# Order of the first loads in a hybrid attention layer: one weight block in two transfers, token rows ahead of the last two blocks, and two small moves in the step schedule

## The chip, the cores and the metric

The kernel runs on one core of a Trainium2 chip. The metric is the device time of one launch in microseconds (us). One execution was also recorded by the hardware profiler; all rows of a trace in this text come from that execution.

The engines are named as in the profile: PE is TensorE (PEld its weight loads, PEq its sequencer), DVE is VectorE, ACT is ScalarE, POOL is GpSimd, SP is SyncE. SP computes nothing here: it only issues transfers, in program order. A transfer that SP issues travels in queue q1; an indirect gather that POOL issues travels in queue q0. Both queues use the same 16 DMA engines.

## What is computed

One inference step of one decoder layer for 512 prompt tokens and 8 decode rows (each with a past of 4096 tokens in paged caches), all in float32:

```python
xn = _rmsnorm(x, norm_pre)
(qa, kvc, kvs, kvw, gn, ga, qd, kvd, krp, gb, ma, mb) = jnp.split(xn @ w_in, IN_OFFSETS, axis=-1)
...
o_a   = gg[..., 0:1] * o_c + gg[..., 1:2] * o_s + gg[..., 2:3] * o_w   # compressed, selected, sliding
o_lat = _mla_attend(q_lat, q_pe, t, c, kr, pos_k)                      # multi-head latent attention
...
pa = (o_a * jax.nn.silu(ga)) @ w_proj_a
pb = (o_b * jax.nn.silu(gb)) @ w_proj_b
h = jax.nn.sigmoid(ma) * pa + jax.nn.sigmoid(mb) * pb
return x + _rmsnorm(h @ w_out, norm_post)
```

For the decode rows the compressed branch averages blocks of 32 cached tokens. The whole compressed cache of those rows, 32 MB, is read for that.

## The kernel before, in words

Every engine has one program written out by hand, and semaphores order the engines. Three stretches matter here.

**Projection, about 0 to 134 us.** The 520 token rows stand transposed in `XG`, as 8 blocks of 128 channels (`k` = 0 to 7). The attention columns of `w_in` are 1976 wide and lie in `W` in two halves of 988; each half has 8 blocks `k` of 128 x 988 words (494 KB), and each block two pieces `n` of 494 columns. A tile is 128 tokens. `project_first` (L957) works on tiles 0 and 1 with the first half: for each `k` it waits for `xg` (`XG` block scaled by DVE in `scale_x`) and for `w_in{k}`, then makes four products of 494 columns. Then `project(u)` (L970) for `u` = 2 to 7 takes one tile and one half each, `u` = 4 to 7 being the second half. A bank is free for the next tile once ACT (`evict`) and DVE (DVE's own `project`, for the first two tiles) have copied it out (`tiles_evicted`). The copy multiplies by 1/rms of the token, which comes from the token rows as such: SP loads them into `xtok` (2 MB) and `xdec`, ACT squares them, and a short chain of DVE and ACT gives `inv_root`. PE starts with two products on zeros (L1060).

SP issues, in this order: `XG` block 0, `W` block 0, `XG` 1 and 2, `W` 1, `W` 2, `XG` 3 and 4, `W` 3, `W` 4, `XG` 5 to 7, `W` 5, `W` 6, `W` 7, then the token rows (L645, L646). After that it waits for `summed` 1, and issues the second half of the weights (L650).

**The gathers, inside the projection.** POOL waits for `w_in7`, and then issues 32 indirect gathers of 1 MB of the compressed cache (L821). There are six slots; gather g+6 waits until DVE has made the first sum of gather g (`summed`, L2065). DVE reduces each gather in three additions (L2065, L2067, L2071; the last raises `sum1`). DVE's order is: eviction of tile 0, gathers 0 and 1, eviction of tile 1, gathers 2 to 7, and so on. PE takes them up in `average(b)` (L1004), which waits for `sum1` of 4(b+1) and stands at fixed places in PE's program: `average(0)` is in tile `u` = 2, `average(1)` in `u` = 3, `average(2)` in `u` = 4. PE works in order, so that a wait in `average` holds all products behind it.

**After the gathers.** POOL gathers rotary keys, SP writes them out again turned (`rope_out`, L662), and only then SP issues `w_qup` and `w_k` (L667, L668), for which ACT waits at L1788 before it copies the columns `ROPE_W` and evicts the transposed queries that PE needs at L1110.

**Attention steps, about 184 to 450 us.** 48 steps `d`, each with two attention units of the prompt. The latent attention of the decode rows is spread over them by hand: `latent_pair(p2, d, d2)` puts the scores of 8 pages at step `d` and of 8 more at `d2`; softmax is at `d2`, the outputs at `d2` + 1. The rotary keys of a pair are loaded to one place (`KRR`) by an ACT transfer, which waits until the pair before has used it (`load_rope`, L1818). `G_at` lists the steps at which PE computes one of 16 gate halves (L1398), eight products of 260 columns.

Of the kernel before, what the change touches and what calls it, by code (L numbers as in the profile page):

```python
# [16 lines left out]
P = 128  # L17
D_MODEL = 1024
SEQ = 512
DEC = 8  # L20
# [13 lines left out]
TILES = SEQ // P  # L34
KM = D_MODEL // P
TOK = SEQ + DEC
# [6 lines left out]
GW = W_ATTN // NG  # L43
# [120 lines left out]
def build(nc, t):  # L164

    ctx = ExitStack()
    with ctx:
# [14 lines left out]
        S = Sems()  # L182
# [10 lines left out]
        W = sb("W", NG * 8 * GW)  # L193
        XG = sb("XG", KM * TOK + 24)
        OA = sb("OA", 5 * 512)
        OB = sb("OB", 5 * 512)
        VV = sb("VV", TILES * 256)
# [6 lines left out]
        rope_rows = nc.dram_tensor("rope_rows", (16 * P, 4 * P), F32, kind="Internal").ap()  # L204
        bank = [ctx.enter_context(nc.psum_tensor(f"bank{i}", [P, 512], F32)) for i in range(8)]
# [35 lines left out]
        xtok, xdec, sqs = c_(4096), c_(1024), c_(1024)  # L241
# [95 lines left out]
        ROPE_APART = (13, 15)  # L337

        def rope_home(p2):
            return PTd[:, :] if p2 in ROPE_APART else KRR[:, 0:512]  # L340

        def rope_landed(eng, p2):
            if p2 in ROPE_APART:
                eng.wait_ge(S["rope_apart"], 16 * (ROPE_APART.index(p2) + 1))
            else:
                eng.wait_ge(S["kr_landed"], 16 * sum(1 for x in range(p2 + 1) if x not in ROPE_APART))

# [67 lines left out]
                C_at[d + 1] = add(d + 1, "slc", r, 0, 512, 4, 64, n, r, False, J_SLC + r)  # L415
                C_at[d + 2] = add(d + 2, "slc", r, 1, 512, 4, 64, n + 1, n, True, J_SLC + r)

        for p2, (d, d2) in enumerate(((0, 1), (3, 4), (6, 7), (9, 10), (12, 13))):
            latent_pair(p2, d, d2)
        for g in range(6):  # L420
            latent_pair(5 + g, 15 + 4 * g, 16 + 4 * g)
            cached(g, 21 if g == 1 else 16 + 4 * g)
        for p2, d in ((11, 39), (12, 41), (13, 43), (14, 45), (15, 47)):
            latent_pair(p2, d, d + 1)
        G_at = {d: i for i, d in enumerate((23, 25, 26, 27, 29, 30, 33, 34, 35, 37, 38, 41, 43, 45, 48, 49))}
        APPLY_at = {d: (i,) for d, i in G_at.items() if i < 14}
        APPLY_at[PAIRS + 1] = (14, 15)
        TURN_IN_7 = {d for d in SOFT_at if d >= 16}
# [148 lines left out]
        def w_part(half, k, n):  # L577
            at = ((half * KM + k) * 2 + n) * GW
            return W[:, at:at + GW]
# [58 lines left out]
        def _(sp):  # L638
            for k in range(KM):
                if k in X_RUNS:  # L640
                    r = X_RUNS.index(k)
                    k2 = (*X_RUNS, KM)[r + 1]
                    sp.dma_start(XG[:, k * TOK:k2 * TOK], t["xT"][:, k * TOK:k2 * TOK]).then_inc(S[f"xT_in{r}"], 16)
                sp.dma_start(W[:, k * 2 * GW:(k + 1) * 2 * GW], t["w_attn"][:, k, 0:2 * GW]).then_inc(S[f"w_in{k}"], 16)
            sp.dma_start(xtok.rearrange("p (t c) -> p t c", t=TILES), t["x"][0:SEQ].rearrange("(t p) c -> p t c", p=P)).then_inc(S["xtok_in"], 16)  # L645
            sp.dma_start(xdec[0:DEC], t["x"][SEQ:TOK]).then_inc(S["xtok_in"], 16)  # L646

            sp.wait_ge(S["summed"], 1)
            for k in range(KM):
# [153 lines left out]
            for i, tl in enumerate(ROWS_DONE):  # L803
                for hf in range(2):
                    sp.wait_ge(S["y"], 2 * i + hf + 1)
                    c = slice(hf * 512, (hf + 1) * 512)
# [130 lines left out]
        def _(pe):  # L937
# [19 lines left out]
            def project_first():  # L957
                for k in range(KM):
                    pe.wait_ge(S["xg"], k + 1)
                    pe.wait_ge(S[f"w_in{k}"], 16)  # L960
                    for tl in range(2):
                        for n in range(2):
                            mm = pe.matmul(bank[2 * tl + n][:, 0:GW], XG[:, k * TOK + tl * P:k * TOK + (tl + 1) * P],
                                           w_part(0, k, n), start=(k == 0), stop=(k == KM - 1))
                        if k == KM - 1:
                            mm.then_inc(S["p1"], 1)
                    if k == 2:
                        pages()
# [87 lines left out]
                mm.then_inc(S["group_dec"], 1)  # L1056

            pe.wait_ge(S["pe_zero"], 1)
            for _ in range(2):
                pe.matmul(bank[7][:, :], VV[:, 0:P], VV[:, 0:512], start=True, stop=True)  # L1060
            project_first()
            for u in range(2, 8):
                project(u)
# [25 lines left out]
            for b in range(4):  # L1089
                for e in range(2):  # L1090
                    n = 4 * e + b
                    mm = pe.matmul(bank[5][32 * e:32 * e + 32, 0:P], QZraw[:, n * 64 + 32 * e:n * 64 + 32 * e + 32], KcT[:, n * P:(n + 1) * P],
                                   start=(b == 0), stop=(b == 3))
# [15 lines left out]
            for k in range(4):  # L1109
                mm = pe.matmul(bank[2][32 * k:32 * k + 32, :], kcBD[:, (k // 2) * 32:(k // 2 + 1) * 32], qTraw[:, k * 512:(k + 1) * 512],  # L1110
                               start=True, stop=True)
# [5 lines left out]
            for n in range(10, 16):  # L1117
                c, w = GROUPS[n]
                mm = pe.transpose(bank[7][0:w, P + 8 * n:P + 8 * n + 8], projD[0:DEC, c:c + w], ident8)
# [63 lines left out]
            for b in range(4):  # L1183
                for e in range(2):
                    n = 4 * e + b
# [463 lines left out]
        def _(act):  # L1649
# [159 lines left out]
            def load_rope(p2):  # L1809
                if p2 == ROPE_APART[0]:  # L1810
                    act.wait_ge(S["do_ps"], sum(1 for c in chunks if c["kind"] != "mla"))
                elif p2:
                    act.wait_ge(S["ds"], mla[p2 - 2 if p2 > ROPE_APART[0] else p2 - 1]["q"] + 1)
                else:
                    act.wait_ge(S["pooled"], 8)
                    act.wait_ge(S["rope_out0"], 128)
                    act.wait_ge(S["rope_out1"], 128)
                act.dma_start(rope_home(p2), rope_rows[p2 * P:(p2 + 1) * P]).then_inc(S["rope_apart" if p2 in ROPE_APART else "kr_landed"], 16)  # L1818

            group_copied(act, 15)  # L1820
            for i in range(4):
# [1141 lines left out]
```

## Time and profile before

| | |
|---|---|
| median of 3 runs | 666.37 us (666.15 to 666.65) |
| profiled execution, device time | 666.29 us |
| its span in the trace | 664.5 us |
| PE busy | 650.8 us, 98% of the span |
| DVE busy | 446.0 us, 67% |
| ACT busy | 214.4 us, 32% |
| DMA, mean | 270 GB/s over the span; 396 GB/s in the first 60 us |

The span starts at the first recorded instruction; the device time has 1.8 us around it. A row of the timeline reads: start, duration, engine, line, operation, tensors, count, and in brackets how long the engine was idle before and what ended it.

### The profile page before, as it was taken

Reading aid. Unit: us, or ns where it says so; the run is one execution under the profiler, and the core shown is the slowest. Engines: PE = TensorE matmul, PEld = TensorE weight load, DVE = VectorE, ACT = ScalarE, POOL = GpSimd, SP = SyncE. Lnnn points to the kernel's source line nnn. Section 1 sums busy time; section 2 is a strip of 40 time slices with the busy share of each in tenths; the row PEclk is TensorE's granted clock in tenths of the full one; section 3 lists DMA queues with packets and bytes.
Section 4 is the critical chain, followed back from the end, with each engine's and each line's share of the span. In section 5 each row is a group of like instructions: output and inputs, shape, how many; then the busy total and the mean of one; then the engine's idle time right before and its main releaser. Section 6 shows DMA issues by size and latency. Waiting matters only on the chain.

```text
span 664.5 us, 15351 instructions
## 1 busy us (share of the span) xinstructions
PE 650.8 (98%) x5771; PEld 433.3 (65%) x5771; DVE 446.0 (67%) x1234; ACT 214.4 (32%) x586; POOL 77.6 (12%) x89
## 2 busy tenths in 40 slices
PE   8999999999999998999999999999999999999996
PEld 3444444463466775778777676688788888886443
DVE  2198799676677778866575664637585757648866
ACT  0311321686445455544453542421011111010221
POOL 0344334126000000220201000000000000000010
PEclk9999999999999999999999999999999999999998
DMA  8999999999989999978759789975411112018011
GB/s 332 417 425 422 423 427 403 353 379 273 366 277 381 400 399 412 408 276 326 279 177 373 276 318 359 406 270 222 159 64 64 64 49 78 1 70 343 3 64 63
DMA packets 67587, 179.44 MB, mean 270 GB/s; under 512 B 7513, under 2 KB 16498, under 8 KB 60218
## 3 DMA queue, kind: packets, MB, share of 16 engines
q1 hardware_dynamic: 56088, 125.14, 51.2%
q0 software_dynamic: 8640, 48.90, 18.2%
q10 hardware_dynamic: 2786, 4.42, 1.8%
q8 instruction: 46, 0.75, 0.4%
q14 instruction: 27, 0.22, 0.1%
HBM read 169.38 MB, written 12.72 MB: 274 GB/s over the span
## 4 chain that ended last, share of the span: by engine, by line
PE 88%; DVE 5%; DMA 3%; ACT 2%; issue 1%; SPq 1%; DVEq 0%; ACTq 0%
PE bank L1561 20%; PE bank L978 12%; PE bank L1398 9%; PE bank L1612 7%; PE bank L1259 5%; PE bank L1382 4%; PE bank L1285 4%; PE bank L1269 4%; PE bank L1367 4%; DMA projP<-x 3%; PE bank L1590 2%; PE bank L1142 2%; PE bank L1332 2%; PE bank L1342 1%; PE bank L1220 1%
## 5 line engine op out<-in xcount | busy, mean ns | idle before, releaser
L978 PE MATMUL bank<-W,XG 128*128 128x494 f32 x192 | 83.6, 580 | 0.7 <-DVE projP L1998 0.7
L1871 ACT ACTIVATE projP<-bank,projP 128x128 f32<-128x128 f32 (+3 forms) x96 | 49.8, 525 | 38.5 <-DVE projP L2354 37.8
L2657 DVE TENSOR_TENSOR projP<-projP,bank 128x260 f32<-128x260 f32 x81 | 32.6, 422 | 42.4 <-PE bank L1561 41.6
L1398 PE MATMUL bank<-W 128*128 128x260 f32 x256 | 60.3, 389 | 0.0
L1661 ACT ACTIVATE projP<-bank 128x128 f32<-128x128 f32 (+5 forms) x87 | 33.4, 392 | 82.2 <-PE bank L1561 47.7
L978 PEld LDWEIGHTS bank<-W,XG 128*128 128x128 f32 x192 | 35.2, 192 | 36.5 <-issue 35.0
L1398 PEld LDWEIGHTS bank<-W 128*128 128x128 f32 x256 | 47.3, 190 | 10.6 <-issue 3.5
L1661 ACT ACTIVATE W<-bank 128x512 f32<-128x512 f32 (+2 forms) x69 | 40.2, 582 | 38.3 <-PE bank L1021 13.3
L2354 DVE CUSTOM_DVE_ANT_0 bank<-bank,maskb 128x128 f32<-128x128 f32 (+3 forms) x96 | 45.6, 509 | 8.0 <-PE bank L1259 7.1
L1259 PE MATMUL bank<-W 64*128 64x128 f32 (+7 forms) x192 | 46.0, 466 | 0.7 <-ACT projP L1871 0.7
L821 POOL DMA_INDIRECT ring<-cmp,idxi x32 | 38.6, 1208 | 67.8 <-DVE VV L2065 48.1
L2065 DVE TENSOR_TENSOR VV<-ring 128x1024 f32<-128x1024 f32 x32 | 39.1, 1222 | 7.6 <-DMA ring<-cmp,idxi 5.2
L881 POOL TENSOR_TENSOR ring<-XG,OB 128x512 f32<-128x512 f32 x3 | 3.8, 1270 | 300.7 <-DVE XG L2755 300.7
L1561 PE MATMUL bank<-ring 128*128 128x260 f32 x168 | 38.2, 383 | 0.0
L1269 PE MATMUL bank<-cst,projP 128*128 128x128 f32 x240 | 36.7, 280 | 0.3
L1561 PEld LDWEIGHTS bank<-ring 128*128 128x128 f32 x168 | 31.8, 190 | 5.3 <-issue 0.4
L1561 PE MATMUL bank<-W 128*128 128x260 f32 x144 | 34.6, 383 | 0.0
L1952 ACT ACTIVATE projP<-projP 128x260 f32<-128x260 f32 x28 | 11.3, 420 | 71.0 <-DVE projP L2657 70.9
L1269 PEld LDWEIGHTS bank<-cst,projP 128*128 128x128 f32 x240 | 26.7, 140 | 9.7 <-issue 5.0
L1999 DVE TENSOR_SCALAR projP<-projP,sm 128x128 f32<-128x128 f32 (+3 forms) x64 | 28.6, 447 | 2.3
L1561 PEld LDWEIGHTS bank<-W 128*128 128x128 f32 x144 | 27.2, 190 | 4.1
L1612 PE MATMUL bank<-ring,W 128*128 128x512 f32 x64 | 28.3, 592 | 0.0
(479 smaller groups left out, 1163.6 us busy)
## 6 DMA issues: line engine op xcount, KB each, us to landing
ring<-latent SPq DMA_DIRECT2D x168, 256.0 KB, 4.9
XG<-latent SPq DMA_DIRECT2D x56, 256.0 KB, 4.4
W<-w_gate SPq DMA_DIRECT2D x12, 1024.0 KB, 5.8
W<-w_attn SPq DMA_DIRECT2D x16, 494.0 KB, 12.2
W<-latent SPq DMA_DIRECT2D x20, 256.0 KB, 5.3
rope_rows<-ring SPq DMA_DIRECT2D x16, 256.0 KB, 4.4
ring<-win SPq DMA_DIRECT2D x8, 512.0 KB, 7.7
ring<-w_out SPq DMA_DIRECT2D x2, 2048.0 KB, 11.8
```

The source lines that it names most:

```text
L821: pool.indirect_dma_start(out=dst, out_offset=None, in_=src, in_offset=bass.IndirectOffsetOnAxis(ap=rows, axis=0)).then_inc(sem, 16)
L978: mm = pe.matmul(bank[2 * (u % 2) + n][:, 0:GW], XG[:, k * TOK + tl * P:k * TOK + (tl + 1) * P], w_part(half, k, n), start=(k == 0), stop= ...
L1259: pe.matmul(bank[x % 2][:, 0:width], q, kk, start=True, stop=True).then_inc(S["s"], 1)
L1269: mm = pe.transpose(pt_bank(u)[:, kb * P:(kb + 1) * P], Pb[u % 4][:, kb * P:(kb + 1) * P], ident)
L1398: mm = pe.matmul(bank[6][:, 0:HALF], gate_w[g % 2][:, at:at + P], X2[:, k * TOK + hf * HALF:k * TOK + (hf + 1) * HALF], start=(k == 0), st ...
L1561: mm = pe.matmul(pair_bank(v, name)[:, 0:HALF], stationary(a, kk), moving(b, kk), start=(kk == 0), stop=(kk == inner - 1))
L1612: mm = pe.matmul(bk[:, lo:hi], lhs, rhs, start=(kk == 0), stop=(kk == 3))
L1661: return act.activation(dst, src, ACT.Copy, scale=scale)
L1871: act.activation(Pb[u % 4][:, 0:w], bank[u % 2][:, 0:w], ACT.Exp, bias=NMp[:, u:u + 1], scale=-1.0, accum_out=RSp[:, u:u + 1]).then_inc(S[ ...
L2065: dve.tensor_tensor(sum4, x[:, 0:1024], x[:, 1024:2048], ALU.add).then_inc(S["summed"], 1)
L2354: dve.tensor_tensor_reduce(bank[u % 2][:, 0:w], bank[u % 2][:, 0:w], maskb[:, 512 - w:512], -1.0, 1e38, ALU.add, ALU.min, NMp[:, u:u + 1]) ...
L2657: dve.tensor_tensor(out, a, pair_bank(v, product)[:, 0:HALF], ALU.add).then_inc(S["z_by_dve"], 1)
```

## The change

Four edits. (1) `W` block 0 is loaded as two transfers of 247 KB, the second with a semaphore of its own (`apart_in`, which also takes over the counts of `rope_apart`); `project_first` makes the two products with the first piece, waits, and makes the two with the second. (2) The token rows are issued between `W` 5 and `W` 6 instead of after `W` 7. (3) The second product on zeros has 256 columns instead of 512. (4) The second half of latent pair 2 moves from step 7 to step 8 (its softmax to step 8 and its outputs to step 9), and gate half 13 from step 45 to 46.

```diff
-                eng.wait_ge(S["rope_apart"], 16 * (ROPE_APART.index(p2) + 1))
+                eng.wait_ge(S["apart_in"], 16 * (ROPE_APART.index(p2) + 2))
...
-        for p2, (d, d2) in enumerate(((0, 1), (3, 4), (6, 7), (9, 10), (12, 13))):
+        for p2, (d, d2) in enumerate(((0, 1), (3, 4), (6, 8), (9, 10), (12, 13))):
...
-        G_at = {d: i for i, d in enumerate((23, 25, 26, 27, 29, 30, 33, 34, 35, 37, 38, 41, 43, 45, 48, 49))}
+        G_at = {d: i for i, d in enumerate((23, 25, 26, 27, 29, 30, 33, 34, 35, 37, 38, 41, 43, 46, 48, 49))}
...
-                sp.dma_start(W[:, k * 2 * GW:(k + 1) * 2 * GW], t["w_attn"][:, k, 0:2 * GW]).then_inc(S[f"w_in{k}"], 16)
-            sp.dma_start(xtok.rearrange("p (t c) -> p t c", t=TILES), t["x"][0:SEQ].rearrange("(t p) c -> p t c", p=P)).then_inc(S["xtok_in"], 16)
-            sp.dma_start(xdec[0:DEC], t["x"][SEQ:TOK]).then_inc(S["xtok_in"], 16)
+                if k == 6:
+                    sp.dma_start(xtok.rearrange("p (t c) -> p t c", t=TILES), t["x"][0:SEQ].rearrange("(t p) c -> p t c", p=P)).then_inc(S["xtok_in"], 16)
+                    sp.dma_start(xdec[0:DEC], t["x"][SEQ:TOK]).then_inc(S["xtok_in"], 16)
+                if k == 0:
+                    sp.dma_start(W[:, 0:GW], t["w_attn"][:, 0, 0:GW]).then_inc(S["w_in0"], 16)
+                    sp.dma_start(W[:, GW:2 * GW], t["w_attn"][:, 0, GW:2 * GW]).then_inc(S["apart_in"], 16)
+                else:
+                    sp.dma_start(W[:, k * 2 * GW:(k + 1) * 2 * GW], t["w_attn"][:, k, 0:2 * GW]).then_inc(S[f"w_in{k}"], 16)
...
-                    for tl in range(2):
-                        for n in range(2):
-                            mm = pe.matmul(bank[2 * tl + n][:, 0:GW], XG[:, k * TOK + tl * P:k * TOK + (tl + 1) * P],
-                                           w_part(0, k, n), start=(k == 0), stop=(k == KM - 1))
-                        if k == KM - 1:
+                    for tl, n in ((0, 0), (1, 0), (0, 1), (1, 1)) if k == 0 else ((0, 0), (0, 1), (1, 0), (1, 1)):
+                        if (k, tl, n) == (0, 0, 1):
+                            pe.wait_ge(S["apart_in"], 16)
+                        mm = pe.matmul(bank[2 * tl + n][:, 0:GW], XG[:, k * TOK + tl * P:k * TOK + (tl + 1) * P],
+                                       w_part(0, k, n), start=(k == 0), stop=(k == KM - 1))
+                        if k == KM - 1 and n == 1:
                             mm.then_inc(S["p1"], 1)
...
-            for _ in range(2):
-                pe.matmul(bank[7][:, :], VV[:, 0:P], VV[:, 0:512], start=True, stop=True)
+            for width in (512, 256):
+                pe.matmul(bank[7][:, 0:width], VV[:, 0:P], VV[:, 0:width], start=True, stop=True)
```

## Rows read from the trace of the kernel before

**Rows 1.** The page: span, and busy time of each engine.
```profile
span 664.5 us, 15351 instructions
PE 650.8 (98%) x5771; PEld 433.3 (65%) x5771; DVE 446.0 (67%) x1234; ACT 214.4 (32%) x586; POOL 77.6 (12%) x89
```
**Rows 2.** Busy time by stretch (stretch, its length, then each engine), 60 to 130 us.
```profile
60.00:130.00 70.00, 70.00 (x351) 32.04 (x349) 59.30 (x98) 24.89 (x55) 23.57 (x20) 1.00 1.01 402
```
**Rows 3.** The chain of waits that ended last, first 60 us.
```profile
8.05 17.59 DMA projP<-x
```
**Rows 4.** PE's timeline after the first two tiles.
```profile
34.06 11.85 PE L978 MATMUL bank<-W,XG 128*128 128x494 f32 x28 [0.70 <-DVE projP L1998]
```
**Rows 5.** PE instructions of two lines, first 35 us: ns min/median/max, first and last start.
```profile
L1060 PE MATMUL bank<-VV x4: 1061/1061/1222, 1.5 to 4.2; 128*128 128x512 f32 x4
...
L963 PE MATMUL bank<-W,XG x64: 575/577/768, 5.5 to 32.8; 128*128 128x494 f32 x64
```
**Rows 6.** SP's transfers: `XG` block 0 to landing; `W` 0 to 7, issue and landing.
```profile
XG<-xT SPq DMA_DIRECT2D x1, 260.0 KB, 3.0
...
L644 SPq DMA_DIRECT2D W<-w_attn x8: 417/479/707, 1.2 to 6.9; - x8
...
DMA to landing us min/median/max: 4.2/9.7/13.1
```
**Rows 7.** DMA queues (packets, MB, share): 23.5 to 24, 24 to 38, 38 to 62 us.
```profile
q1 hardware_dynamic: 49, 0.16, 79.4%
q0 software_dynamic: 8, 0.07, 32.2%
...
q0 software_dynamic: 794, 5.85, 100.2%
...
q0 software_dynamic: 927, 6.72, 66.6%
```
**Rows 8.** Timeline: the first gather, SP's second half of the weights.
```profile
20.87 1.01 POOL L821 DMA_INDIRECT ring<-cmp,idxi  x1 [18.14 <-DMA W<-w_attn]
...
35.07 4.38 SPq L650 DMA_DIRECT2D W<-w_attn  x8
```
**Rows 9.** Issue to landing: gather 7 (issued at 37.83 us), gather 11 (at 48.32).
```profile
ring<-cmp,idxi POOLq DMA_INDIRECT x1, 10.4
...
ring<-cmp,idxi POOLq DMA_INDIRECT x1, 15.3
```
**Rows 10.** Timeline: last addition of gather 7, `average(1)`, gather 11, `average(2)`.
```profile
54.26 0.42 DVE L2071 TENSOR_TENSOR KRR<-VV 128x256 f32<-128x256 f32 x1
...
56.55 0.41 PE L1011 MATMUL bank<-OA,cst 128*32 128x256 f32 x2
...
63.68 1.23 DVE L2065 TENSOR_TENSOR VV<-ring 128x1024 f32<-128x1024 f32 x1 [1.26 <-DMA ring<-cmp,idxi]
...
71.42 0.40 PE L1011 MATMUL bank<-KRR,cst 128*32 128x256 f32 x1
```
**Rows 11.** Timeline: last addition of gather 19, `average(4)`.
```profile
92.19 0.42 DVE L2071 TENSOR_TENSOR KRR<-VV 128x256 f32<-128x256 f32 x1
...
94.84 0.41 PE L1011 MATMUL bank<-OA,cst 128*32 128x256 f32 x2
```
**Rows 12.** Timeline: `w_qup` issued, ACT's first copy of it, PE behind it.
```profile
126.66 0.66 SPq L667 DMA_DIRECT2D ring<-w_qup  x1
...
138.56 0.73 ACT L1661 ACTIVATE KRR<-ring 128x256 f32<-128x256 f32 x2
...
140.88 1.06 PE L1110 MATMUL bank<-W,XG 128*32 128x512 f32 x8 [0.16 <-ACT XG L1738]
```
**Rows 13.** The transfer issued right behind `w_k`, at 127.85 us: to landing.
```profile
ring<-const SPq DMA_DIRECT2D x1, 512.0 KB, 15.1
```
**Rows 14.** Timeline: outputs in step 8, the gate half of step 45.
```profile
213.94 0.86 PE L1285 MATMUL bank<-projP,W 128*32 128x128 f32 x24 [0.46 <-DVE projP L2362]
...
422.23 3.77 PE L1398 MATMUL bank<-W 128*128 128x260 f32 x16
```

More of the change, by code:

```diff
@@ L1817, in load_rope @@
                     act.wait_ge(S["rope_out1"], 128)
-                act.dma_start(rope_home(p2), rope_rows[p2 * P:(p2 + 1) * P]).then_inc(S["rope_apart" if p2 in ROPE_APART else "kr_landed"], 16)
+                act.dma_start(rope_home(p2), rope_rows[p2 * P:(p2 + 1) * P]).then_inc(S["apart_in" if p2 in ROPE_APART else "kr_landed"], 16)
             group_copied(act, 15)
```

## Prediction

> **What bounds the kernel now.** I read the page first: PE is busy for 98% of the span [rows 1], so a change gains only where PE waits or starts late, and costs wherever it makes PE wait. Busy time by stretch says the same of the part this change touches: from 60 to 130 us PE is busy for 70.00 of 70.00 us [rows 2]. Then the chain of waits for the first 60 us: its longest piece is the transfer of the token rows, issued at 8.05 and awaited for 17.59 us, to 25.6 [rows 3]. Behind it come five squares, the root, and the first evictions, and PE's timeline shows the price: 0.70 us idle before tile 2, released by DVE's eviction [rows 4]. With the start of the first real product at 5.51 [rows 5] these are the two places where PE is late. Last I read the DMA queues and the gathers, since the token rows are put ahead of something that others wait for.
>
> **Edits 1 and 3, the start.** `XG` block 0 landed at 0.76 + 3.0 = 3.8, `W` block 0 at 1.2 + 4.2 = 5.4 [rows 6]. Half of the block should land half of that interval earlier, at about 4.6. The shorter second product on zeros leaves PE free in time: each of the 4 instructions has 1061 ns [rows 5], half the columns save some 0.43 us in each of two, so they end at 4.4 rather than 5.25. PE starts up to 0.86 us earlier. But the products of 512 zeros at 1061 ns and the later ones of 494 columns at 577 ns [rows 5] stand for the two levels of the clock, 1.2 and 2.4 GHz, although the record of the granted clock shows full speed throughout; the first real product, 768 ns, still has the change in it. So the level rose just after 5.5, and what is done before that goes at half speed: the gain is 0.43 (bounds 0 and 0.86).
>
> **Edit 2, what it gains.** The token rows are no longer behind `W` 6 and 7, 1.0 MB, 2.4 us at the 0.418 MB/us of a full queue (5.85 MB in 14 us, [rows 7]). `inv_root` comes before tile 0 is done, and the 0.70 us go [rows 4]. Blocks 6 and 7 land 5.1 us later, at 23.9 and 25.1, and PE wants them at about 26 and 29: covered. Without anything else the change would gain 0.43 + 0.70 = 1.1 us.
>
> **Edit 2, what it costs.** POOL starts its gathers only when `W` 7 has landed: it landed at 6.9 + 13.1 = 20.0 [rows 6], and the first gather was issued at 20.87, released by it after 18.14 us [rows 8]. The token rows are 2.13 MB, 2.13 / 0.418 = 5.1 us of the queue. `W` 7 then lands at 25.1 and the first gather is issued at 26.0. Its first bytes were seen 2.8 us after the issue (8 packets of q0 between 23.5 and 24, [rows 7]), so they come at about 28.8. Before, the token rows filled q1 during just this latency. Now nothing is behind `W` 7: SP waits for `summed` 1, which waits for the first gather. The DMA engines stand idle from about 24.2 to 28.9, 4.7 us, in a stretch where they were full.
>
> The Trainium skill (DMA: Bandwidth & Descriptors, Queues, rings and completion order) says that each DMA engine consumes a ring's descriptors in ring order, and that completion need not be in order. By the landings, 4.2 to 13.1 us after issue in the order of issue, the trace agrees with the first part; if the engines overtook one another, `W` 7 would land earlier than I say. The same page (Specifications) gives about 1 us to the first byte on the POOL path. This trace has 2.8 us, and the measurement decides; by 1 us, as an estimate from that page, the hole would be 2.9 instead of 4.7 us, and the time 668.9.
>
> **Who is short of data.** Gather g is in when q0 has moved (g + 1) x 1.05 MB. Before, q0 moved 0.07 + 5.85 = 5.92 MB by 38 us, alone, and from then 6.72 / 24 = 0.280 MB/us beside the second half of the weights [rows 7]. Test on gather 7: 8.39 MB at 38 + 2.47 / 0.280 = 46.8; it landed at 37.83 + 10.4 = 48.2 [rows 9], 1.4 later. Gather 11: 61.8, landed at 63.6 [rows 9], 1.8 later. Now after the change. q0 starts at 28.9. Gather 0 lands at 28.9 + 2.5 + 1.4 = 32.8, DVE's first addition ends at 34.0, and SP issues the second half of the weights then instead of at 35.07 [rows 8]. Their bytes began 2.9 us after that issue, so the sharing begins at 36.9 with 3.34 MB moved.
> - Gather 7: 36.9 + 5.05 / 0.280 + 1.4 = 56.3. DVE's three additions take 2.4 us (1.23 the first, 0.42 the last, [rows 10]), so `sum1` 8 is there at 58.7. `average(1)` ran at 56.55, with 1.9 us to spare since 54.68 [rows 10]. PE reaches it at 55.4 and waits 3.3 us: 2.1 us later than before.
> - Gather 11: 36.9 + 9.24 / 0.280 + 1.8 + 2.4 = 74.1, against `average(2)` at 71.42 [rows 10]. PE comes at 73.6 and waits again: **2.7 us later** than before. Both gains of PE at the start are inside this wait and count nothing.
> - From there the gathers are late by the whole hole, 4.7 us, and PE by 2.7. `average(4)` had 94.84 - 92.61 = 2.2 us to spare [rows 11]; 4.7 - 2.7 = 2.0 fits in it just. The cost of a miss is what is missing, 0 to 0.5 us; I take 0.
>
> **The next in line.** SP issues `w_qup` and `w_k` after the rotary rows, which come after the gathers, at 126.66 [rows 12]; now 4.7 later. ACT copied from it at 138.56 with no wait in the row, and PE waited 0.16 us at L1110 for the evictions that follow on ACT [rows 12], so there is no cover on that side. The transfer right behind `w_k` landed at 127.85 + 15.1 = 142.95 [rows 13], half a megabyte later, so `w_k` landed not long before 138.5. If just then, ACT waits 4.7 - 2.7 = 2.0 us; if 2 us earlier, nothing. Being nearer to the first, I take **1.5 us**. Queued behind ACT's wait are the evictions of the transposed queries, and PE waits for them. What follows is timed by PE again.
>
> **Edit 4.** Before, PE waits 0.46 us in step 8 for DVE [rows 14], while step 7 carries eight more pages. Moving them (1.3 us of PE) fills that hole and leaves step 7 with 1.3 us less cover for the softmax of its wide units. Outputs and the slot of those pages come a step later, and the next rotary load starts some 4 us later with one step less to land. Gain 0.5, loss 0.5: I take 0. Gate half 13 is 3.8 us of PE work in step 45 [rows 14]; the neighbours have it as cover or not, both steps being full of PE work. Its weights are long in, and SP's loads don't count it. 0, between -0.2 and 0.2.
>
> **Sum.** 2.7 + 1.5 = 4.2 us on the execution of 666.29 us, whose span is 664.5: 670.5. The median of the runs, 666.37, is 0.1 above that execution, so nothing is to be corrected.
>
> **The rivals.** (a) The hole costs at the two averages alone, since `w_k` was in early enough, or the second wait is smaller: 666.3 + 2.1 to 2.7 = 669.0. For it: no row shows when `w_k` landed. (b) The hole is short, since the gather's first bytes come sooner on an empty queue, as after the page's 1 us: +2.6, 668.9. Against it: 2.8 us in this trace. (c) On the other side: the gathers keep up. If POOL's gathers start so early, or DVE has so much in hand, that gather 7 is added by 55.4 and gather 11 by 70.3, PE keeps its 1.1 us: 665.2. It decides if the gathers come less than 0.7 us later than before at gather 7; for it speaks that all the bytes are the same and PE had 1.9 us to spare; against it, that DVE waited for gather 11 already, 1.26 us [rows 10]. (d) The waits just eat the gains: 666.3 +- 1.3, no change. (e) The clock: PE stands for 3.3 us before `average(1)`, more than anywhere in the record after the start. If the level falls to 1.2 GHz, each microsecond at it costs half of one. Only what exceeds the 0.5 us that PE comes early to `average(2)` counts, and it takes the place of the wait for `w_k`: up to 3 us more, 671 to 674. The Trainium skill (TensorE: Matmul & The Clock Gate, the HAM clock gate) says that the slow state is the default and activity lifts it; by that rule the fall is possible, and rows 5 agree for the start.
>
> **Chances.** Forecast 0.55 (its own range 669.3 to 672.0), (a) 0.15, (b) 0.05, (c) 0.12, (d) 0.06, (e) 0.07. The range leaves out (c), most of the low part of (d) and the far end of (e): 667.0 to 673.0. A measurement of this kernel can tell about 0.2%, 1.3 us, from no change: faster 0.12, same 0.07, slower 0.81.
>
> **What would show it.** In the trace after: no q0 or q1 bytes between 24.3 and 28.7; `W` 7 landing at about 25 and the first gather at 26; tile 2 following tile 1 on PE without the 0.70 us; PE idle 3 us before L1011 at 58.7 and again shortly at 74; ACT idle before its first copy from `w_qup`. If the first gather starts near 21, or DMA is full around 26, the prediction is wrong at its root. If PE doesn't wait at L1011, the model of the sharing is wrong; if L1110 is late by as much as `average(2)`, the 1.5 us are.

## The result, and the profile after

The changed kernel took 674.62 us, the median of 4 runs (673.43 to 676.06), beside 666.51 us for the kernel before (4 runs): a ratio of 1.0103, 95% interval 1.0066 to 1.014. The profiled execution took 673.43 us, with a span of 671.6 us: 7.1 us more than before, where I forecast 4.2. By the medians it is 8.1 us. The profiled execution is the shortest of the four; the other three have a lower granted clock (0.992 or 0.993 on the mean, beside 0.996) and no trace.

The page first: the span, and PE's share one point lower. PE is busy for 651.9 us rather than 650.8 [rows 1], so most of the 7.1 us is waiting and some is work at a lower speed.

```profile
span 671.6 us, 15352 instructions
...
PE 651.9 (97%) x5771; PEld 433.9 (65%) x5771; DVE 446.7 (67%) x1234; ACT 214.3 (32%) x586; POOL 77.7 (12%) x89
```

The summary of PE's waits (line waited for: us in total, times, longest) says where it stood. The first two lines are new.

```profile
PE bank L1017 <- DVE KRR L2077: 3.4, 1, 3.4
PE bank L1116 <- ACT XG L1744: 3.2, 1, 3.2
```

Lines behind the edits are numbered 5 or 6 higher than before. Busy time by stretch (the last three columns are granted clock, DMA share and GB/s) shows the cause of both:

```profile
20.00:24.00 4.00, 4.00 (x11) 1.89 (x10) 0.00 (x0) 0.64 (x1) 0.00 (x0) 1.00 1.03 374
24.00:28.00 4.00, 4.00 (x11) 1.83 (x10) 0.00 (x0) 3.91 (x8) 1.17 (x2) 1.00 0.13 53
28.00:32.00 4.00, 4.00 (x11) 1.77 (x10) 1.03 (x6) 1.41 (x4) 3.08 (x4) 1.00 0.92 305
32.00:36.00 4.00, 4.00 (x11) 1.90 (x10) 3.05 (x5) 1.34 (x2) 2.71 (x3) 1.00 0.96 360
60.00:130.00 70.00, 69.50 (x348) 31.95 (x341) 61.08 (x89) 24.28 (x55) 25.09 (x20) 1.00 1.00 410
```

The DMA engines ran dry between 24 and 28 us, as forecast, but they were also thin on both sides of it. The kernel before moved 415, 407, 428 and 430 GB/s in these four stretches; the difference is 2.35 MB, 5.6 us of a full queue, where I had counted 4.7. The timelines of POOL, SP, ACT and PE follow the delay down:

```profile
26.53 1.00 POOL L826 DMA_INDIRECT ring<-cmp,idxi  x1 [23.79 <-DMA W<-w_attn]
...
59.61 0.41 PE L1017 MATMUL bank<-OA,cst 128*32 128x256 f32 x2 [3.44 <-DVE KRR L2077]
...
75.05 0.40 PE L1017 MATMUL bank<-KRR,cst 128*32 128x256 f32 x1 [0.50 <-DVE OA L2077]
...
132.50 0.65 SPq L672 DMA_DIRECT2D ring<-w_qup  x1
...
145.24 0.72 ACT L1667 ACTIVATE KRR<-ring 128x256 f32<-128x256 f32 x2 [3.13 <-DMA ring<-w_k]
...
147.56 1.93 PE L1116 MATMUL bank<-W,XG 128*32 128x512 f32 x8 [3.22 <-ACT XG L1744]
```

Against [rows 8, 10, 12]: the first gather is 5.66 us later, `average(1)` 3.06, `average(2)` 3.63, the issue of `w_qup` 5.84, and L1116 6.68. The eight products at L1116 last 1.93 us instead of 1.06, and the granted clock says why. It is at 0.50, the 1.2 GHz level, once PE has stood idle for 3.2 us:

```profile
144.00:146.00 2.00, 0.35 (x4) 0.11 (x1) 1.97 (x9) 0.76 (x3) 0.40 (x1) 1.00 1.02 303
146.00:148.00 2.00, 0.44 (x4) 0.23 (x8) 0.76 (x2) 1.98 (x5) 2.00 (x4) 0.73 0.98 390
148.00:150.00 2.00, 2.00 (x11) 0.43 (x4) 0.00 (x0) 1.99 (x4) 0.15 (x1) 0.50 1.03 421
```

The transfers of 24 to 38 us in 40 slices of 0.35 us show the hole itself, with the first bytes again in the slice from 28.2:

```profile
GB/s 395 181 34 0 0 0 0 0 0 0 0 0 328 164 164 421 445 374 374 351 375 258 281 304 304 374 351 328 281 375 398 421 445 375 421 445 421 351 375 442
```

At the start the first product comes 1.20 us earlier than in [rows 5], and yet the gain is gone before the third block:

```profile
4.31 4.88 PE L969 MATMUL bank<-W,XG 128*128 128x494 f32 x8
9.42 6.87 PE L969 MATMUL bank<-W,XG 128*128 128x494 f32 x16 [0.23 <-DMA W<-w_attn]
...
17.09 16.75 PE L969 MATMUL bank<-W,XG 128*128 128x494 f32 x40
33.68 2.65 PE L984 MATMUL bank<-W,XG 128*128 128x494 f32 x6
```

The last 40 products of `project_first` began at 16.61 before and begin at 17.09 now. The 0.70 us of idle time before tile 2 [rows 4] are gone, so tile 2 is 0.38 us early in all.

The books of the profiled pair: +3.63 to `average(2)`, which stays to 133 us; +3.05 at the wait for `w_k` (L1116 is 6.68 late); +1.07 by the low clock behind it (the row at 170.12 was at 162.37, 7.75 in all); -0.6 later on. That is 7.1.

### The profile page after: what moved, and what is told of

Read it like the earlier page. It is cut to its first block, busy times and chain, and to the rows that moved or that the text cites. A ratio compares the mean times of both kernels' runs of the same rounds, so it can differ in the third digit from the quotient of the medians.

```text
span 671.6 us, 15352 instructions
## 1 busy us (share of the span) xinstructions
PE 651.9 (97%) x5771; PEld 433.9 (65%) x5771; DVE 446.7 (67%) x1234; ACT 214.3 (32%) x586; POOL 77.7 (12%) x89
## 4 chain that ended last, share of the span: by engine, by line
PE 73%; DMA 12%; DVE 9%; issue 2%; SPq 2%; ACT 1%; POOL 0%; DVEq 0%; POOLq 0%; ACTq 0%
PE bank L1567 20%; PE bank L1404 9%; PE bank L1618 7%; DMA ring<-cmp,idxi 7%; PE bank L1265 5%; PE bank L1388 4%; PE bank L1291 4%; PE bank L1275 4%; PE bank L1373 4%; DVE VV L2071 3%; DMA W<-w_attn 2%; PE bank L1596 2%; DMA ring<-w_k 2%; PE bank L1148 2%; PE bank L1348 2%
## 5 line engine op out<-in xcount | busy, mean ns | idle before, releaser
L984 PE MATMUL bank<-W,XG 128*128 128x494 f32 x192 | 83.5, 579 | 0.0
L969 PE MATMUL bank<-W,XG 128*128 128x494 f32 x64 | 28.5, 602 | 0.2 <-DMA W<-w_attn 0.2
```

The lines of the kernel that those rows point to most:

```text
L984: mm = pe.matmul(bank[2 * (u % 2) + n][:, 0:GW], XG[:, k * TOK + tl * P:k * TOK + (tl + 1) * P], w_part(half, k, n), start=(k == 0), stop= ...
```

## The experiments

Each kernel ran 6 to 13 times, beside the kernel before on the same chip. The medians of the kernel before were 665.67 us beside the first four rows of the table, 666.76 for the next four, 666.52 for the next four and 665.35 for the last four. The ratio is not the quotient of the two medians, and where they disagree the interval decides.

| kernel | median us | ratio | 95% interval |
|---|---|---|---|
| before, edit 2 alone | 671.64 | 1.0094 | 1.0056 to 1.0131 |
| after, edit 2 undone | 665.61 | 1.0005 | 0.9978 to 1.0032 |
| after, gathers from block 5 | 665.48 | 0.9995 | 0.9978 to 1.0012 |
| before, edit 4 alone | 666.18 | 0.9999 | 0.9978 to 1.0020 |
| before, gathers late | 671.40 | 1.0075 | 1.0049 to 1.0101 |
| before, edits 1 and 3 | 667.53 | 1.0008 | 0.9988 to 1.0029 |
| after, evictions first | 671.12 | 1.0069 | 1.0045 to 1.0093 |
| after, both waits filled | 673.48 | 1.0097 | 1.0077 to 1.0117 |
| after, again | 673.25 | 1.0088 | 1.0056 to 1.0119 |
| after, both waits filled, again | 672.91 | 1.0110 | 1.0046 to 1.0173 |
| after, one wait filled | 673.06 | 1.0088 | 1.0062 to 1.0114 |
| before, rows early, gathers from block 5, latent pair 2 moved | 666.02 | 0.9991 | 0.9962 to 1.0021 |
| the same, evictions first | 665.08 | 1.0001 | 0.9990 to 1.0011 |
| before, evictions first | 665.46 | 1.0004 | 0.9988 to 1.0019 |
| after, evictions first, again | 671.13 | 1.0088 | 1.0062 to 1.0115 |
| the same, first wait filled | 669.97 | 1.0070 | 1.0057 to 1.0083 |

**Which edit.** Edit 2 alone, put into the kernel before:

```
+                if k == 6:
+                    sp.dma_start(xtok..., t["x"][0:SEQ]...)
+                    sp.dma_start(xdec[0:DEC], t["x"][SEQ:TOK])
                 sp.dma_start(W[:, k * 2 * GW:...], t["w_attn"][:, k, 0:2 * GW])
-            sp.dma_start(xtok..., t["x"][0:SEQ]...)
-            sp.dma_start(xdec[0:DEC], t["x"][SEQ:TOK])
```

> The kernel before with edit 2 alone: token rows ahead of weight blocks 6 and 7, the first block in one transfer, both zero products of 512 columns, edit 4 left out. Theory (the hole in the DMA queues carries the loss, since the gathers wait for weight block 7): first gather issued near 26, average(1) near 59, average(2) near 75, the wait for w_k 3 us, and the time some 7.5 to 8 us above before, 674. Rival 1 (the split first block and its small packets delay the early blocks and so carry a part): 2 us or more less than that, 672 or below. Rival 2 (the loss comes from edit 4): within 1 us of before.

Taken out of the changed kernel, with all else left in:

> The changed kernel with edit 2 undone: the token rows are again issued behind weight block 7; the split first block, the short zero product and edit 4 stay. Theory (edit 2 carries the whole loss, edit 4 gives back the 0.6 us that the trace of after shows between 262 and 443 us, the start gives nothing): 665.8, that is 0.5 below before. Rival (the split first block costs, since block 1 landed 0.7 us later): 667 to 668. If it stays above 671, edit 2 isn't the cause.

Edit 4 alone, `(6, 7)` to `(6, 8)` and gate half `45` to `46`:

> The kernel before with edit 4 alone (second half of latent pair 2 from step 7 to step 8, gate half 13 from step 45 to step 46). Theory (the 0.6 us that after gives back between 262 and 443 us are PE's idle time before step 8's pages): 0.5 us below before, 665.9. Rival (they come from the shifted phase of the loads, not from edit 4): 0 within 0.2.

Edits 1 and 3 alone:

> The kernel before with edits 1 and 3 alone: first weight block in two transfers, second zero product of 256 columns. Theory (the level of the clock rises at the same time whatever is done before it, and block 1 lands 0.4 to 0.7 us later than PE wants it): the first real product starts near 4.3, the ninth at 9.4 to 9.6 rather than 9.02, tile 2 on PE is as late as before, and the time is within 0.4 us of before. My prediction's term: 0.43 us below before. Rival (small packets delay all of the start): 1 us or more above before.

Edit 2 alone costs 6.0 us by the medians; without it the changed kernel is at 665.61, level with before. I had expected 7.5 to 8 us from edit 2, and had given 672 or below as the sign that the split first block carries a part. 671.64 is below that line, but the other two runs speak against it: with the split block and edit 2 undone nothing is lost, and edits 1 and 3 alone measure +0.8 us within an interval that holds 0. A share of some tenths of a microsecond isn't excluded. My 0.43 us of gain isn't there. Edit 4 measures nothing: the 0.6 us of the profiled pair are below what the runs tell. The trace of edits 1 and 3 shows block 1 awaited, and its first product (the ninth of all) at 10.29, later than the 9.4 to 9.6 that I expected:

```profile
4.44 5.14 PE L968 MATMUL bank<-W,XG 128*128 128x494 f32 x8
10.29 6.87 PE L968 MATMUL bank<-W,XG 128*128 128x494 f32 x16 [0.71 <-DMA W<-w_attn]
...
17.96 16.75 PE L968 MATMUL bank<-W,XG 128*128 128x494 f32 x40
```

**Is it the hole?** The changed kernel, with one number changed: POOL's gathers wait for block 5, which is issued ahead of the token rows.

```
-            pool.wait_ge(S["w_in7"], 16)
+            pool.wait_ge(S["w_in5"], 16)
```

> The changed kernel, and POOL's first gather waits for weight block 5, which is issued ahead of the token rows, and no longer for block 7. All the data and the order on SP's queue stay. Theory (the loss is the hole): gathers are issued from about 16, no stretch without bytes, average(1) and average(2) run without a wait, w_k lands early enough, the time 665 to 666. Rival (token rows ahead of blocks 6 and 7 are dear by themselves, or sharing the engines with the gathers makes blocks 6 and 7 and the token rows late): PE waits at L969 or at the first eviction, and the time is 667 to 670.

And from the other side, the kernel before with its old order, and gathers that start late:

```
-            pool.wait_ge(S["w_in7"], 16)
+            pool.wait_ge(S["xtok_in"], 32)
```

> The kernel before, and POOL's first gather waits for the token rows in place of weight block 7. Order and sizes of all transfers stay; only the gathers start about 5.6 us later, when the queue has run dry. Theory (the lateness of the gathers is the whole cause, whatever order the token rows have): a stretch without bytes from about 25.5 to 28.5, PE waits 3 to 4 us at average(1), and the time is 5.5 to 8 us above before, like the kernel with edit 2 alone. Rival (the order of the token rows itself costs): less than 3 us above before.

The first takes the whole loss away (665.48 us), the second brings in 4.6 us of it with no transfer moved, below the 5.5 that I gave as the least. Its first gather went at 25.53, 1.0 us earlier than in the changed kernel; whether that is all of the difference isn't shown. From 24 to 32 us the two rows of the changed kernel above make 1.43 MB; with gathers from block 5 the queues stay full, and its first gather is out at 18.92 (not at 16, as expected: the row has it released by the last indices from DVE, not by the weights):

```profile
24.00:28.00 4.00, 4.00 (x11) 1.79 (x10) 0.00 (x0) 3.91 (x7) 1.83 (x2) 1.00 1.01 423
28.00:32.00 4.00, 4.00 (x11) 1.90 (x10) 1.02 (x6) 1.58 (x5) 0.00 (x0) 1.00 1.02 429
```

With the old order and late gathers they run dry in the same place, and PE waits at `average(1)` (stretches, then PE's timeline):

```profile
24.00:28.00 4.00, 4.00 (x11) 1.90 (x10) 0.00 (x0) 3.18 (x5) 1.95 (x2) 1.00 0.20 41
28.00:32.00 4.00, 4.00 (x11) 1.83 (x10) 0.89 (x5) 2.77 (x7) 2.99 (x4) 1.00 0.96 344
```

```profile
58.36 0.41 PE L1011 MATMUL bank<-OA,cst 128*32 128x256 f32 x2 [2.66 <-DVE KRR L2071]
```

So the late start of the gathers, with the dry stretch that it leaves, and not the order of the token rows, is the cause.

**The wait for `w_k`.** PE doesn't need `w_k` at L1116; it needs evictions that stand behind it on ACT. They were put ahead:

```
+            act.wait_ge(S["cst_in"], 48)
+            group(10, bank[1]); group(12, bank[2]); group(14, bank[0])
             job_landed(act, J_W1)
             act.wait_ge(S["pooled"], 8)
             (three copies from w_qup and w_k)
-            act.wait_ge(S["cst_in"], 48)
-            group(10, bank[1]); group(12, bank[2]); group(14, bank[0])
```

> The changed kernel, and ACT evicts the transposed groups 10, 12 and 14 ahead of its copies from w_qup and w_k instead of behind them. The copies still wait for the transfer. Theory (the transfer of w_k is late, but what PE waits for at L1116 is only the evictions queued behind ACT's wait): the 3.2 us at L1116 go and the 1.1 us of low clock with them; ACT's copies end near 146.4, before PE wants them near 147.6; 4 us below after's time, so 4 above before, which is the cost of the averages alone. Rival (PE needs the transfer itself right behind): the wait shows up at the first product from w_qup, and the time is within 1 us of after's, 7 to 8 above before.

4.4 us above before; measured again later it was 5.8 above (below, where I had expected 4 to 5), and the changed kernel was 8.1 and 6.7 above in its two measurements. The intervals overlap; the middle of the one pair is 2.3 us below that of the other, somewhat less than the 3 us of the wait. The trace is plain: L1116 starts at 145.05 with no wait; ACT's copies, now behind, start at 145.65, 0.4 us later than in the changed kernel, and PE doesn't notice.

```profile
145.05 1.06 PE L1116 MATMUL bank<-W,XG 128*32 128x512 f32 x8
```

**The clock.** Both waits were filled with products of no use, 22 and 20 of them, 117 ns each in the trace:

```
             if b == 1:
                 pe.wait_ge(S["mpe"], 1)
+                for i in range(22):
+                    pe.transpose(bank[6][:, 384:512], ident, ident)
+            pe.wait_ge(S["sum1"], 4 * (b + 1))
...
+            for i in range(20):
+                pe.transpose(bank[7][:, 384:512], ident, ident)
             pe.wait_ge(S["prep_by_dve"], BY_DVE["kcbd"])
```

> The changed kernel with work for PE inside its two long waits: 22 transposes of the identity into unused columns of a bank ahead of average(1), and 20 ahead of the wait at L1116 (135 to 150 ns each by the rows of L1027, so about 3.1 and 2.8 us against waits of 3.44 and 3.22). They compute nothing that is used. Theory (the clock falls to 1.2 GHz in or after these waits, at L1116 in the profiled run of after, and that costs 1.0 to 1.3 us there): the granted clock stays at full speed over 144 to 152 us, L1116 takes 1.06 us again, and the time is 1 to 1.5 us below after's, that is about 6.5 above before, with less spread from run to run. Rival (the low clock at L1116 isn't due to PE standing idle): no change, 8 above before.

> The changed kernel once more, unaltered, so that the variants stand beside it on one chip. Expected: 6.5 to 8 us above before, spread over 2 to 3 us from run to run, and low granted clock in a stretch behind average(1) or behind the wait at L1116, not always the same one.

> The changed kernel with both waits of PE filled by transposes, beside the changed kernel itself on one chip. Theory (the low clock costs a microsecond or more on top of the waits): no stretch of low granted clock, 1 to 1.5 us below the changed kernel, spread under 1.5 us. Rival (the lost clock is hidden in the next wait, since transfers set the time there): within 0.5 us of the changed kernel.

> The changed kernel with the 20 transposes ahead of the wait at L1116 alone; the wait ahead of average(1) stays empty. Theory: a clock that falls at average(1) is paid for by the wait for w_k, which ends by the transfers; a clock that falls at L1116 is paid in full. So filling L1116 alone gives all that filling both gives, 1 to 1.5 us below the changed kernel. Rival (the fall at average(1) costs by itself): about half of that.

Filling both keeps the clock at 1.00 behind both waits, in both profiles. The times are 672.91 beside 673.25 us for the changed kernel on the same chip, and 673.06 with the second wait alone filled: nothing that can be told apart, and not the 1 to 1.5 us that I expected. Two of the six executions with both waits filled took 679.89 and 680.9 us at a mean granted clock of 0.990; they have no trace.

The profile with the second wait alone filled is of its slowest execution, 680.24 us, and it shows the largest cost of the clock on record. PE did its 20 transposes, stood idle for 2.86 us more, since `w_k` came at 147.66, and then ran at the low level to about 159 us (PE's timeline, then two stretches):

```profile
149.98 1.93 PE L1118 MATMUL bank<-W,XG 128*32 128x512 f32 x8 [2.86 <-ACT XG L1746]
```

```profile
150.00:152.00 2.00, 2.00 (x9) 0.31 (x10) 0.00 (x0) 1.97 (x5) 0.00 (x0) 0.50 1.02 408
154.00:156.00 2.00, 2.00 (x3) 0.67 (x2) 0.33 (x4) 1.98 (x5) 0.00 (x0) 0.50 1.13 341
```

These products are 9.10 us later than in the kernel before, and the row that was at 162.37 there comes at 175.62, 13.25 later: 4.1 us by the clock, where the changed kernel's first profile has 1.07. My rival, that the lost clock hides in the next wait, has a trace on its side too. In the kernel with edit 2 alone the clock fell at `average(1)` (PE's timeline, then two stretches with the granted clock third from the end):

```profile
60.52 0.64 PE L1012 MATMUL bank<-OA,cst 128*32 128x256 f32 x2 [3.98 <-DVE KRR L2072]
...
77.84 0.40 PE L1012 MATMUL bank<-KRR,cst 128*32 128x256 f32 x1
```

```profile
58.00:62.00 4.00, 1.48 (x10) 0.67 (x11) 2.58 (x4) 0.00 (x0) 1.27 (x1) 0.60 1.01 421
62.00:66.00 4.00, 4.00 (x7) 1.68 (x6) 2.69 (x4) 0.28 (x1) 1.27 (x1) 0.55 1.00 418
```

`average(2)` is 6.42 us later than before, not 3.63 (0.9 of the difference was there at `average(1)` already), and from there PE has no long wait: it reaches the products behind L1116's at 149.51, where before reached them at 143.10, with the lateness of `w_k` inside that of PE. The second profile of the changed kernel is in between: 0.80 and 0.78 behind `average(1)`, then only 0.97 us of wait at L1116 and no fall there. Of the 2.25 us by which that wait is shorter, 1.06 are PE's later arrival; the other 1.19 are that the evictions came earlier in that execution. So only a part of what is missing from the second wait was taken by the clock at the first. That execution still took 676.01 us, for another reason: against the first profile 5.1 us were lost between 403 and 413 us, first 2.83 us of idle time with nothing in the profile that PE waited for, then work at a granted clock of 0.63 and 0.52. Why PE stood there is not known.

```profile
407.62 0.63 PE L1388 MATMUL bank<-ring,projP 128*32 128x256 f32 x5 [2.83 <-issue]
```

To take the cover of the `w_k` wait away, the wait at `average(1)` was filled in the kernel with evictions first:

> The changed kernel with ACT's evictions ahead of the copies, once more, as the mate on the same chip of the kernel with PE kept busy ahead of average(1). Expected: 4 to 5 us above before, with a stretch of low clock behind average(1) in the profile.

> The changed kernel with ACT's evictions ahead of the copies and 22 transposes of the identity on PE ahead of average(1). No later wait covers what is lost at the first average. Theory (the low clock there costs 1 us or more; in b_rows_early it put average(2) 2.8 us later than after's): 1 to 2 us below its mate, 3 above before. Rival (the gathers time average(2) anyway, 1.1 us wait there with full clock): within 0.5 us of its mate.

669.97 against 671.13 us: 1.2 us less, with intervals that overlap. The two traces say more: from 62 to 66 us the granted clock is 0.50 in the unfilled one, 1.00 in the filled.

```profile
62.00:66.00 4.00, 4.00 (x6) 1.60 (x5) 2.69 (x4) 0.15 (x1) 1.27 (x1) 0.50 1.01 424
...
62.00:66.00 4.00, 4.00 (x11) 1.89 (x10) 2.51 (x4) 0.14 (x1) 1.26 (x1) 1.00 1.02 425
```

PE's timelines, unfilled, then filled:

```profile
60.35 0.64 PE L1017 MATMUL bank<-OA,cst 128*32 128x256 f32 x2 [3.85 <-DVE KRR L2077]
...
78.11 0.40 PE L1017 MATMUL bank<-KRR,cst 128*32 128x256 f32 x1
```

```profile
60.93 0.41 PE L1019 MATMUL bank<-OA,cst 128*32 128x256 f32 x2 [1.54 <-DVE KRR L2079]
...
76.27 0.40 PE L1019 MATMUL bank<-KRR,cst 128*32 128x256 f32 x1 [0.40 <-DVE OA L2079]
```

From the first average to the second PE takes 17.76 us in the one and 15.34 with 0.40 of wait in the other: 2.8 us of work more at the low level, of which 1.84 us are left at the second average.

**Can the gains be had?** With the hole closed, the 0.70 us before tile 2 should show.

> The kernel before with edit 2, the first gather released by weight block 5 rather than 7, and latent pair 2 moved as in edit 4; the first block in one transfer, no short zero product. Theory: the 0.7 us before tile 2 go, and the 0.5 us before the pages of step 8; no long wait comes in: 1.1 us below before. Rival (blocks 6 and 7 and the token rows share the engines with the gathers and come too late): PE waits for weight blocks 6 or 7 or at the first eviction, and the time is equal to before or above.

They don't: the median is 0.5 us below before, in an interval that holds 0. The trace says where they went: `average(1)` ran at 55.62, 0.93 us early, and at L1111 only 0.09 us of it were left.

```profile
138.46 0.72 ACT L1662 ACTIVATE KRR<-ring 128x256 f32<-128x256 f32 x2 [0.91 <-DMA ring<-w_k]
...
140.79 1.07 PE L1111 MATMUL bank<-W,XG 128*32 128x512 f32 x8 [0.99 <-ACT XG L1739]
```

In the kernel before, ACT took up `w_k` at 138.56 with no wait in the row, straight from other work. In the trace of edit 4 alone, whose loads are those of the kernel before, ACT did wait for it:

```profile
138.87 0.72 ACT L1661 ACTIVATE KRR<-ring 128x256 f32<-128x256 f32 x2 [0.35 <-DMA ring<-w_k]
```

So `w_k` lands just when ACT wants it in the kernel before too, with next to no slack, and a gain ahead of it is lost there. My 1.5 us had been a guess between slack and none. That led to the last pair:

> The kernel before, and ACT evicts the transposed groups 10, 12 and 14 ahead of its copies from w_qup and w_k. Theory (w_k lands just when ACT wants it, PE waits 0.16 us): nothing of note, 0 to 0.3 us below before. Rival (the copies, 1.9 us of ACT, now come after the evictions and PE waits for them at the first product from w_qup): up to 1 us above.

> The kernel before with edit 2, gathers released by weight block 5, latent pair 2 moved, and the evictions of groups 10, 12 and 14 ahead of the copies from w_qup and w_k. Theory (in b_rows_w5 PE came 0.9 us early to L1111 and waited 0.99 us there, so w_k's transfer took the gain): that wait goes and the time is 1.0 to 1.5 us below before. Rival (PE needs the late transfer itself): within 0.3 us of before, like b_rows_w5.

The wait is gone (L1111 at 140.47 with none), but 665.08 us beside 665.35 is no gain that can be told, and my 1.0 to 1.5 us are not there. In this execution the first 24 products took 11.42 us against 10.19 in the trace of its sister, which has the same start, and `average(1)` ran at 56.37. So a gain of 0.7 us at the start is no larger than what the start varies by. A gain of up to 0.1%, the lower end of the interval, isn't excluded.

## Why the prediction was wrong, step by step

The forecast was 670.5 us and the median 674.62, 4.1 more. The profiled pair shows 2.9 of them: 0.93 at the averages, 1.55 at the wait for `w_k` and 1.07 by the clock, which the sum left out, less 0.6 later on. The other 1.2 lie between the profiled execution and the median; they come with a lower mean clock, and no trace shows where.

- **Direction and mechanism: right.** `W` 7 landed at 9.58 + 16.09 = 25.67 (forecast 25.1), the first gather went at 26.53 (26.0), PE waited 3.44 us at `average(1)` (3.3) and again 0.50 at `average(2)`, and ACT waited for `w_k`. Tile 2 came without the 0.70 us.
- **The step that failed by the most: the size of the wait for `w_k`.** I took 1.5 us of 0 to 2.0, "4.7 - 2.7". It measured 3.05 on PE. `w_qup` was issued 5.84 us late, and ACT's first copy came 12.74 us after that issue rather than 11.90, another 0.84; less the 3.63 that PE had lost, that is 3.05. So three things were too small: the slack that I allowed, 0.5 us, wasn't there; the difference of the two terms was 2.2 and not 2.0; and the longer transfer was not in the sum at all. Why it took longer isn't shown. It varies: the same interval is 11.84 us in the second profile of the changed kernel and 14.47 in the one of 680.24 us.
- **The hole: 4.7 us, measured 5.6 us' worth of bytes.** I had a full queue up to 24.2 and from 28.9. The bytes came back sooner, at 28.2, 1.7 us after the first gather's issue. (The Trainium skill, DMA: Bandwidth & Descriptors, Specifications, has about 1 us there; this trace lies between it and the 2.8 us of the kernel before, and the measurement decides.) But the last transfers before the hole and the first 8 us of gathers after it ran thin, at 374, 305 and 360 GB/s instead of 415 to 430. Gather 7's last sum came at 59.55 rather than 58.7, and the cost to `average(2)` was 3.63 rather than 2.7.
- **The clock: rival (e), put at one wait alone, and at nothing in the sum.** I gave it 0.07 and 671 to 674 us, at `average(1)`. In the profiled run it fell at L1116, behind my under-sized wait, and cost 1.07 us there. In other executions it fell at `average(1)`. With both waits filled the median didn't move by more than the runs can tell, so what it adds to the median stays open: 1.07 us in one trace, 4.1 in the slowest one, and in the kernel with edit 2 alone 2.4 us more work between the two averages, behind which no wait for `w_k` was left.
- **Edits 1 and 3: 0.43 us, measured none.** The first half block came early, but the level of the clock, which I had rising just after 5.5 us, rose later: by their durations, 1181, 1029 and 1012 ns, the first three products of the changed kernel still ran at the low one, to about 6.9 us, and the first eight took 4.88 us where they had taken 3.51. Block 1 also came later: PE waited for it to 9.42, where it had started on it at 9.02. The saved time went to the slow level first, and to that landing then.
- **Edit 4: 0, right.** Its step 8 wait went in the trace, and the time didn't move.

The Trainium skill (TensorE: Matmul & The Clock Gate, HAM oscillation — how this bites in real kernels) says that a wait for data can put PE back to the slow clock and that the cost then comes on top of the wait. The traces agree where nothing behind covers the cost, with 2.8 us more work between two averages.

## What to carry to other kernels

Before a transfer is moved ahead in a queue, look for who waits for the one that it overtakes: a semaphore that only orders the issue of the next queue turns a reordering into a dry stretch, and one changed number (gathers from block 5) undid it. A wait's cost is not complete until the next two waits by the same late stream are sized, and the slack of each is looked for rather than guessed. A saved microsecond ahead of a landing, or of a wait that covers it, is no saving. And a profile is one execution: two of the same kernel put the clock's fall at different waits, and one of them lost 5.1 us at 403 us, where the other lost nothing.

## What the hardware showed that I had not expected

- **The same idle time doesn't always cost the clock.** PE stood 3.44 us before `average(1)` in the profiled run of the changed kernel and the granted clock stayed at 1.00; in the same kernel's other profile it stood 3.19 us and the clock was at 0.80 and 0.78 for the stretches from 58 and from 62 us. With 3.98 us it was at 0.60 and 0.55, with 2.66 at 0.69 and 0.89, and with only 2.17 (second wait filled) at 0.81 and 0.77. Here is the first stretch in the two profiles of the changed kernel:

```profile
58.00:62.00 4.00, 2.39 (x13) 1.09 (x14) 2.59 (x4) 0.28 (x1) 1.27 (x1) 1.00 1.01 420
...
58.00:62.00 4.00, 2.47 (x12) 1.09 (x13) 2.63 (x4) 0.28 (x1) 1.27 (x1) 0.80 1.02 424
```

- **The clock also falls while PE is busy.** In the profiles of edit 4 alone and of the changed kernel with edit 2 undone it was at 0.50 from about 136 to 139 us, with PE busy in the whole stretch from 134 to 142, among other things with transposes and small products. In none of the other sixteen profiles did it fall between 130 and 140 us. In the trace of edit 4 the products from 135.85 on took 1.2 us longer for it than in the kernel before. One stretch of it:

```profile
137.00:138.00 1.00, 1.00 (x10) 0.73 (x9) 1.00 (x4) 1.00 (x3) 0.00 (x0) 0.50 0.95 397
```

- **Transposes can hold the clock.** In seven profiles PE stood 2.17 us or longer before `average(1)`, and the clock fell in six of them. With 22 transposes there, and 0.20 to 1.54 us of idle time left, it stayed at 1.00 in all three. With 20 transposes and 2.86 us left, ahead of L1118, it fell. The Trainium skill (TensorE: Matmul & The Clock Gate, Part 4: PE-mode transpose) says that transposes don't count as busy for the clock in the same way; the three filled waits show no sign of it.
- **After the dry stretch the queue is thin for about 8 us.** The gathers moved 305 and then 360 GB/s where the full queue has 430. It is so in all ten profiles with late gathers (270 to 344 GB/s from 28 to 32 us, 356 to 406 from 32 to 36), and not with gathers from block 5 (429 and 426). I have no experiment on why.
